# Loading half of the input tiles from ScalarE's queue instead of SyncE's in a one-core encoder layer

## The reference

```
h = rmsnorm(x, norm1_g)              # x * rsqrt(mean(x*x) + eps) * g, by token
z = h @ w_in + b_in                  # 1024 x 2312, one projection for both mixers
att = window_sink_attention(z parts) # 8 heads, window of two chunks of 64
ml  = mlstm_chunkwise(z parts)       # 4 heads
x = x + concat(rmsnorm(att), rmsnorm(ml)) @ w_out
x = x + conv_ffn(rmsnorm(x, norm2_g))
return rmsnorm(x, final_g)
```

## Time and profile before

| what | value |
|---|---|
| median of 3 runs | 1046.57 us (1046.47 to 1046.63) |
| the profiled execution: its own time | 1046.44 us |
| its span, first to last instruction | 1044.7 us |
| TensorE matmul busy | 1020.6 us, 98% of the span |
| VectorE busy | 727.7 us, 70% |
| ScalarE busy | 500.1 us, 48% |
| HBM traffic | 102 GB/s over the span |

### The profile page before, as it was taken

How to read it: one execution, slowest core, us unless ns; L and a number is a source line. 1 busy time by engine, 2 the same in 40 slices (tenths; PEclk the granted TensorE clock), 3 DMA queues, 4 the chain that set the end, 5 groups by cost and what they waited for, 6 DMA issues and landing times.

```text
span 1044.7 us, 13267 instructions
## 1 busy us (share of the span) xinstructions
PE 1020.6 (98%) x4933; PEld 845.2 (81%) x4933; DVE 727.7 (70%) x1153; ACT 500.1 (48%) x940; POOL 74.6 (7%) x80
## 2 busy tenths in 40 slices
PE   5999999999989999899999999999999999999997
PEld 4888888888778888788888888888888888888886
DVE  5352555651585557998777777777777788995796
ACT  7532435444572322665445445454454644444473
POOL 5010222220240000000000000000000000000000
PEclk9999999999999999999999999999999999999999
DMA  7226101111233224233123132231230999125104
GB/s 217 50 67 153 40 26 41 41 37 26 55 110 120 81 81 121 82 100 121 61 82 101 61 99 83 81 101 61 81 101 21 348 355 384 41 91 190 52 1 162
DMA packets 108640, 107.75 MB, mean 103 GB/s; under 512 B 13330, under 2 KB 81032, under 8 KB 108576
## 3 DMA queue, kind: packets, MB, share of 16 engines
q1 hardware_dynamic: 107040, 103.56, 31.4%
q0 software_dynamic: 1536, 3.34, 1.3%
HBM read 86.93 MB, written 19.96 MB: 102 GB/s over the span
## 4 chain that ended last, share of the span: by engine, by line
PE 92%; DVE 4%; ACT 2%; issue 1%; DMA 1%; POOL 0%; DVEq 0%; ACTq 0%; POOLq 0%
PE pz L1846 19%; PE pz L2143 7%; PE pz L2144 7%; PE pz L2145 7%; PE pd L2143 6%; PE pd L2144 6%; PE pd L2145 6%; PE pd L2167 4%; PE pd L2164 4%; PE pd L2166 4%; PE pz L2167 3%; PE pz L2164 3%; PE pz L2166 3%; PE pd L2074 3%; PE pd L2072 3%; PE pd L2073 3%
## 5 line engine op out<-in xcount | busy, mean ns | idle before, releaser
L1027 ACT ACTIVATE ws_hi<-raw 128x512 fp32r<-128x512 f32 x88 | 52.9, 626 | 102.1 <-PE pz L2145 48.4
L1846 PE MATMUL pz<-h_hi,w_hi 128*128 128x512 f32 x304 | 99.2, 399 | 2.6 <-DVE h_lo L1227 2.5
L1846 PE MATMUL pz<-h_lo,w_hi 128*128 128x512 f32 x304 | 96.7, 391 | 0.0
L1846 PE MATMUL pz<-h_hi,w_lo 128*128 128x512 f32 x304 | 96.3, 390 | 0.0
L2143 PE MATMUL pz<-ht_hi,ws_hi 128*128 128x512 f32 x240 | 93.5, 389 | 2.7 <-DVE u L1627 2.7
L2144 PE MATMUL pz<-ht_lo,ws_hi 128*128 128x512 f32 x240 | 93.4, 389 | 0.0
L2145 PE MATMUL pz<-ht_hi,ws_lo 128*128 128x512 f32 x240 | 93.4, 389 | 0.0
L2143 PE MATMUL pd<-ht_hi,ws_hi 128*128 128x512 f32 x200 | 77.8, 389 | 0.0
L2144 PE MATMUL pd<-ht_lo,ws_hi 128*128 128x512 f32 x200 | 77.8, 389 | 0.0
L2145 PE MATMUL pd<-ht_hi,ws_lo 128*128 128x512 f32 x200 | 77.8, 389 | 0.0
L1644 DVE SCALAR_TENSOR_TENSOR gate<-u,vec,gate 128x1023 f32<-128x1023 f32 (+1 forms) x44 | 56.5, 1283 | 20.0 <-ACT gate L1069 19.3
(11 more groups left out here) (299 smaller groups left out, 2492.7 us busy)
## 6 DMA issues: line engine op xcount, KB each, us to landing
raw<-in_w_up SPq DMA_DIRECT2D x48, 512.0 KB, 4.8
b<-in_w_down SPq DMA_DIRECT2D x49, 256.0 KB, 7.3
act_rows<-gate SPq DMA_DIRECT2D x22, 512.0 KB, 2.7
a<-act_rows SPq DMA_DIRECT2D x44, 256.0 KB, 4.8
raw<-in_w_in SPq DMA_DIRECT2D x14, 512.0 KB, 3.7
x_in<-in_x SPq DMA_DIRECT2D x8, 512.0 KB, 6.0
x_again<-in_x SPq DMA_DIRECT2D x8, 512.0 KB, 4.1
b_raw<-in_w_down SPq DMA_DIRECT2D x14, 256.0 KB, 5.6
```

The costliest lines, as they stand in the source:

```text
L1027: nc.scalar.activation(ws_hi[m][:, :, :], summand(p, i), ACT.Copy).then_inc(s["ws_hi_made"], 1)
L1846: ins = mm(dst[:, h * HALF:(h + 1) * HALF], w[:, c], v[:, h * HALF:(h + 1) * HALF], start=first, stop=last)
```

## The change

The four loads of tiles 4 to 7 are taken out of SyncE's program, where they stood behind the loads of block 1 of w_in. They are put at the head of ScalarE's program, ahead of its wait for the memsets. Sources, destinations, sizes and semaphores of the four loads are the same.

```diff
@@ SyncE @@
                 else:
                     sp.dma_start(dst, w_in_d[:, :, j * P:(j + 1) * P]).then_inc(raw_loaded[b % 2], 16)
-                if b == 1:
-                    load_x(range(NT // 2, NT))
 
             for k in range(NK):
@@ ScalarE @@
         @block.scalar
         def _(act):
 
+            for i in range(NT // 2, NT):
+                act.dma_start(x_in[:, i, :], x_d[i * P:(i + 1) * P, :]).then_inc(tile_loaded[i], 16)
             act.wait_ge(s["mem_made"], 3)
```

## The result

The changed kernel took 1050.95 us (median of 6 runs, 1050.24 to 1052.15) against 1046.97 us of the kernel before in the same runs (1046.47 to 1047.75): a ratio of 1.0038 with a 95% interval of 1.0026 to 1.0050. It is slower by 4.0 us; 3.8 us, or 1050.4, had been forecast.

The account below looks back on a forecast made before the run. TensorE was taken to bound the kernel, its dense stretch started by tile 3's chain. Tile 3 4.5 us later, less 0.7 of waits, other terms 0, gave +3.8: 1050.4 us forecast, range 1046.9 to 1051.8.

Parts of the forecast that it names:

- What sets the start: First 24 us: tile 3's landing at about 9.5 us starts the chain to TensorE's dense stretch at 23.83 us.
- Part 1: SyncE's queue: giving up four issues that hold it 4.87 us gains 0, as its next load waits for VectorE.
- Part 2: Head of ScalarE's program: four issues of about 1.81 us hide in its 2.61 us wait for tile 0; cost 0.
- Part 3: DMA engines at the start: sharing with tiles 4 to 7 lands tile 3 4.5 us later, dense stretch 3.8 later.
- The slack: Chain behind tile 3: waits of VectorE, 0.32 and 0.37 us, would vanish and give back 0.7 us.
- the sum: Start of the dense stretch: 4.5 - 0.7 = +3.8 us, for a median of 1050.4 us; chance 0.62.
- Part 4: TensorE at the start: quick pace expected after half of block 0's first matmuls; cost 0, bounds 0 and +2.5 us.
- Rival (b): Block 0's first half: TensorE's slow pace lasts, up to 2.5 us late, 1051.4 to 1052.9 us; chance 0.12.
- The rule and the row on sharing: DMA queues: round robin by packet, or first issued first as at 80 to 86 us; nearly the same result here.
- Rival (a): Start of ScalarE: table load first, tile 3 at 9.5 to 10.8, 1046.6 to 1047.2 us; 0.24 with similar ways.
- Gains "hidden behind tile 3": GpSimd's queue at the start: gains and gate columns may come about 1 us later, hidden, at no cost.

Follow-up runs that it names:

- e5_one: Kernel before, with only tile 4 loaded from the head of ScalarE's program, the other tiles left on SyncE: ratio 0.9997 (0.9988 to 1.0006).
- e4_two: Kernel before, with only tiles 4 and 5 loaded from the head of ScalarE's program, the others left on SyncE: ratio 1.0015 (1.0006 to 1.0025).
- e11_after_gain: Changed kernel, with the gains loaded by ScalarE's first instruction, ahead of its four tiles: ratio 1.0021 (1.0011 to 1.0031) against the kernel before.
- e1_late: Changed kernel's four ScalarE loads issued only behind the square and root of tile 3: ratio 0.9999 (0.9990 to 1.0008) against the kernel before.
- e6_split: Kernel before, with tiles 1 and 3 loaded from the head of ScalarE's program, tiles 0 and 2 from SyncE: ratio 1.0010 (1.0001 to 1.0019).
- e3_tiny: Kernel before, plus four loads of 8 bytes per partition at the head of ScalarE's program: ratio 0.9999 (0.9990 to 1.0008).
- e8_warm: Kernel before, plus 18 dummy transposes on TensorE ahead of the gains' transpose: ratio 0.9996 (0.9987 to 1.0004).
- e9_gain: Kernel before, with the gains loaded by ScalarE's first instruction instead of from GpSimd's queue: ratio 0.9992 (0.9983 to 1.0001).
- after_again: Changed kernel run once more, unedited: ratio 1.0038 (1.0024 to 1.0051) against the kernel before.
- e7_filled: Changed kernel, plus dummy transposes on TensorE ahead of tiles 1, 2 and 3: ratio 1.0038 (1.0024 to 1.0051) against the kernel before.
- e2_sp8: Kernel before, with all eight tiles loaded in order from SyncE's queue and w_in behind them: ratio 1.0001 (0.9992 to 1.0010).

## Why the prediction was right

**What sets the start.** Right. With tile 3 between 9.5 and 14.3 us, w_hi of block 0 starts 2.7 to 2.9 us after its landing in the kernel before, e5_one, e4_two, e11_after_gain and both profiles of the changed kernel. It is 3.1 in e1_late, with the issues in between, and 3.5 in e6_split, where the late tile 2 stood ahead.

**Part 1, nothing gained on SyncE.** Right: with 4.87 us of issues taken off it, SyncE still issued its next load of w_in only when VectorE was done with block 0. Nor did it come free much sooner: the second load of w_in's block 1 took 6.0 us to issue instead of 2.35, and SyncE was free at 9.4 instead of 10.7.

**Part 2, four issues on ScalarE at no cost.** Right. They took 2.14 us, not 1.81, and the table load came behind them at 2.98; e3_tiny shows the time unchanged with the issues and without the bytes.

**Part 3, the size.** Right within 0.3 us for tiles 1 to 3, and 0.6 us too late for tile 0: they landed at 5.6, 8.7, 11.3 and 14.3 us against the forecast 6.2, 8.9, 11.5 and 14.0. The slack is confirmed from the other side by e8_warm and e9_gain, with 1.0 us there against 0.7. That the 3.85 of after_again meets the sum's 3.8 so closely is partly luck, as two small errors cancel: tile 3 was 4.7 to 4.8 us late and not 4.5, and the waits that vanished gave back 0.75 to 0.85 us and not 0.7.

**Part 4, the pace.** The step "I expect the quick pace to be there after the first half of them. Cost 0" held in one of the two profiles of the changed kernel and failed in the other, where the clock came back after 14 of 24 matmuls and cost about 1 us; it failed in the profile of e11_after_gain too, by 0.9 us. Rival (b) is thus real in single executions, at the lower end of its 1 to 2.5 us, and comes and goes. It is not the main loss (after_again, e7_filled). How much of it is in the median of 4.0 us is not shown.

**The rule and the row on sharing.** The text said that even sharing and order of issue give the same here. They do for the changed kernel, where tile 3 landed behind three of ScalarE's tiles and 0.3 us ahead of the fourth. The Trainium skill's round robin by packet (DMA: Bandwidth & Descriptors, section Queues, rings and completion order) agrees with the halves of 52.5% and 47.7% in the changed kernel, and with those of 50.4% and 49.5% from 5 us on in e11_after_gain. It doesn't explain that ScalarE's first tile there moved nothing until 3.6 us after its issue, which looks more like the earlier trace rows. What in the DMA engines makes it so stays open.

**Rival (a), table load first.** It fell: the table load stood behind the four issues. Its threshold, two of ScalarE's tiles ahead of tile 3 for about 0.2%, fits e4_two (+0.15%).

**Gains "hidden behind tile 3".** True in the changed kernel, where VectorE began only 0.42 us later and TensorE had gaps afterwards. e6_split shows where it stops being true: with tile 3 landed on time and the gains 1.45 us late, the gains set the start.

## What to carry to other kernels

Here a second queue added no bandwidth, as one queue already filled the DMA engines (407 against 401 GB/s); it only gave up the order in which the first would have served. So put what is waited for first ahead on whichever queue, and let what is needed later be issued later: eight tiles in order on one queue cost nothing that could be measured, and neither did the same four issues 10 us later on ScalarE. Before moving a load ask which transfers it will now pass, small ones of other queues among them, and multiply them by the time of one.

## What the runs showed of the hardware

- Two hardware queues filled in step got 52.5% and 47.7% of the DMA engines' time, and 50.4% and 49.5% in e11_after_gain from 5 us on. There, with the first tile of one queue issued 0.62 us later and a small load ahead of it, that queue moved 3 packets from 2 to 5 us, and a landing on the other came 1.9 us sooner.
- A load of 4 KB issued from GpSimd at 1.4 us landed 5.2 to 6.1 us after its issue beside one full queue (e3_tiny, before, e2_sp8) and 5.7 to 6.9 beside two (e4_two, after, e5_one, e6_split). VectorE, which waits for it, started between 7.0 and 8.8 us; with the load issued from ScalarE at 0.8 us it started at 3.4 (e9_gain).
- The granted clock fell to 0.50 at 16.3 and 16.4 us in the two profiles of the changed kernel; in the first, TensorE had been busy 4.9 of the 8 us from 8 to 16. It fell also in e8_warm, at 16.6 us, where the dummy transposes and the tiles' had been followed by a gap of 2.18 us. The column read 1.00 in earlier stretches in which transposes still took 0.21 us, so in these profiles it does not show the slow pace of the start.
